# Inverting unit triangles from 32x32 diagonal blocks on four PE positions, with the sums kept in PSUM and copied out by ScalarE

## The reference

```
def step(S, inp):                                   # rwkv7_scan, one token
    sa = einsum('bhij,bhj->bhi', S, a_t)
    S = S * w_t[:, :, None, :] + sa[..., None] * b_t[:, :, None, :] + v_t[..., None] * k_t[:, :, None, :]
    return S, einsum('bhij,bhj->bhi', S, r_t)

L = where(strict, einsum('bhnid,bhnjd->bhnij', kb, k) * decay, 0.0)      # gated_delta_chunked
t_inv = triangular_solve(eye + L, eye, left_side=True, lower=True, unit_diagonal=True)
u = t_inv @ (v * beta[..., None])
```

## Time and profile before

| | us |
|---|---|
| median of 3 runs | 2749.25 (2746.87 to 2752.73) |
| profiled execution, its own time | 2759.18 |
| its span | 2757.5 |
| PE busy | 2218.6 (80%) |
| DVE busy | 831.5 (30%) |
| ACT busy | 352.2 (13%) |
| mean granted TensorE clock | 0.854 |

### The profile page before, as it was taken

How to read it: one execution, slowest core, us unless ns; L and a number is a source line. 1 busy time by engine, 2 the same in 40 slices (tenths; PEclk the granted TensorE clock), 3 DMA queues, 4 the chain that set the end, 5 groups by cost and what they waited for, 6 DMA issues and landing times.

```text
span 2757.5 us, 37784 instructions
## 1 busy us (share of the span) xinstructions
PE 2218.6 (80%) x16019; PEld 1519.3 (55%) x16019; DVE 831.5 (30%) x1482; ACT 352.2 (13%) x771; POOL 191.2 (7%) x210
## 2 busy tenths in 40 slices
PE   5968888777687888889883998677787888898883
PEld 2445667666574555555552445566674555555551
DVE  1333333433534111111114353456544111111114
ACT  0012111111010111111110013200010111111110
POOL 0000000000000111111110000000000111111110
PEclk9965787877798999999996996588896999999996
DMA  8440233311223999999997152000013999999996
GB/s 296 141 126 7 117 123 127 123 62 62 42 47 143 371 381 370 380 382 366 388 373 280 61 161 84 1 1 9 6 39 126 371 380 374 372 384 370 374 369 243
DMA packets 129926, 581.35 MB, mean 211 GB/s; under 512 B 25890, under 2 KB 33052, under 8 KB 78424
## 3 DMA queue, kind: packets, MB, share of 16 engines
q1 hardware_dynamic: 88368, 496.07, 46.8%
q0 software_dynamic: 28480, 60.42, 6.5%
q10 hardware_dynamic: 12904, 22.35, 2.7%
HBM read 566.42 MB, written 48.30 MB: 223 GB/s over the span
## 4 chain that ended last, share of the span: by engine, by line
PE 62%; DMA 20%; DVE 12%; issue 2%; ACT 1%; PEldq 1%; SPq 1%; PEld 1%; ACTq 0%; DVEq 0%; POOL 0%; POOLq 0%
PE bank L552 57%; DMA ring<-in_exp_w_up 12%; DVE arena L1512 7%; DMA ring<-in_exp_w_down 3%; DMA ring<-in_mod_w 2%; DMA arena<-choice_rows 1%; PE bank L1033 1%; PE bank L656 1%; DMA ring<-in_ev_w_in 1%; DVE mixed L1512 1%; PE bank L1057 1%; DVE arena L1526 1%; DVE arena L1520 1%; PE bank L749 1%; PEld bank L552 0%
## 5 line engine op out<-in xcount | busy, mean ns | idle before, releaser
L552 PE MATMUL bank<-ring,arena 128*64 128x256 f32 (+3 forms) x5168 | 944.2, 447 | 138.5 <-DMA ring<-in_exp_w_up 87.6
L552 PEld LDWEIGHTS bank<-ring,arena 128*64 128x64 f32 (+1 forms) x5168 | 575.2, 158 | 470.4 <-issue 364.6
L552 PE MATMUL bank<-arena 64*64 64x64 f32 (+8 forms) x6176 | 435.2, 257 | 64.0 <-DVE arena L1512 42.1
L552 PEld LDWEIGHTS bank<-arena 64*64 64x64 f32 (+5 forms) x6176 | 376.4, 163 | 103.0 <-DVE arena L1512 41.9
L1526 DVE COPY arena<-bank 128x512 f32<-128x512 f32 (+4 forms) x231 | 151.6, 663 | 562.9 <-PE bank L552 491.2
L552 PE MATMUL bank<-ring,hT 128*128 128x512 f32 (+2 forms) x672 | 265.6, 555 | 12.0 <-DMA ring<-in_ev_w_in 5.7
L1520 DVE SCALAR_TENSOR_TENSOR arena<-bank,arena 128x256 f32<-128x256 f32 (+1 forms) x84 | 40.1, 477 | 683.3 <-PE bank L552 683.3
L552 PEld LDWEIGHTS bank<-ring,hT 128*128 128x128 f32 x672 | 128.1, 199 | 148.7 <-issue 143.0
L2220 POOL DMA_INDIRECT arena<-token_rows,arena x80 | 80.6, 1008 | 940.7 <-PE bank L1033 658.2
L1512 DVE TENSOR_TENSOR arena<-arena 128x1024 f32<-128x1024 f32 (+7 forms) x135 | 124.2, 947 | 48.3 <-DMA arena<-choice_rows 34.7
L552 PE MATMUL bank<-hT,ring 128*128 128x384 f32 x384 | 127.2, 488 | 4.0 <-DVE arena L1512 2.3
(11 more groups left out here) (176 smaller groups left out, 1222.7 us busy)
## 6 DMA issues: line engine op xcount, KB each, us to landing
ring<-in_exp_w_gate SPq DMA_DIRECT2D x128, 1024.0 KB, 10.0
ring<-in_exp_w_up SPq DMA_DIRECT2D x128, 1024.0 KB, 9.6
ring<-in_exp_w_down SPq DMA_DIRECT2D x128, 1024.0 KB, 10.1
ring<-in_mod_w SPq DMA_DIRECT2D x48, 1024.0 KB, 10.2
ring<-in_od_w_in SPq DMA_DIRECT2D x14, 1024.0 KB, 9.9
arena<-choice_rows POOLq DMA_DIRECT2D x4, 3072.0 KB, 14.4
ring<-in_ev_w_in SPq DMA_DIRECT2D x10, 1024.0 KB, 14.8
arena<-arena ACTq DMA_DIRECT2D x12, 672.0 KB, 10.6
```

The lines of the kernel that those rows point to most:

```text
L552: return nc.tensor.matmul(out, lhsT, rhs, start=start, stop=stop, **kw)
```

## The change

Up to width 32 the inverse is now kept as 32x32 diagonal blocks: `low`, 128 partitions by 2 x 4 x 32, T and its transpose. Its products are 32x32 matmuls, 16 for four heads and four quarters of the partitions, and the four quarters sit on four positions of PE. Level 0 is two sums in PSUM (identity by a 128x256 matmul, plus the triangle's blocks by multiplying with a small identity), masked by VectorE. From level 1 on the sum T + join stays in PSUM (one identity matmul puts T there at level 1, the joins accumulate), and ScalarE copies it out to `low` at levels 1 to 4, so that VectorE's add is gone; VectorE's mask is half as wide. The level 32 to 64 becomes a corner of its own, as 64 to 128 was: it has no mask, one product, one join, and copies. Since tt and the new t64 are filled by blocks, POOL clears both whole, and VectorE copies the blocks of `low` into them; ScalarE writes the new corner for group 0, VectorE for group 1.

```diff
-LEVELS = 7
+LOW_LEVELS = 5
+M_STEPS, J_STEPS, T_STEPS = 6, 7, 8
+Q = 32
...
             def invert(inv, n, dirs):          # tensor program
...
+                for g in range(2):
+                    out = bank[2 + g][:, 0:8 * Q].rearrange("p (k h n) -> p k h n", k=2, h=4)
+                    pe.wait_ge(inv.sem("nt_ready", g), n + 1)
+                    mm(bank[2 + g][:, 0:8 * Q], C["ident"], small_ident.unsqueeze(1).broadcast_to([P, 8, Q]), True, False, **acc)
+                    for h in range(4):
+                        for r in QUARTERS:
+                            mm(out[r, 0, h, :], inv.nt[g][r, h, r], small_ident[r, :], False, True, **acc)
+                    for h in range(4):
+                        for r in QUARTERS:
+                            last = mm(out[r, 1, h, :], small_ident[r, :], inv.nt[g][r, h, r], False, True, **acc)
+                    last.then_inc(inv.sem("join_ready", g), 1)
+                for k in range(1, LOW_LEVELS):
                     for g in range(2):
+                        pe.wait_ge(inv.sem("t_ready", g), T_STEPS * n + k)
+                        if k == 1:
+                            mm(bank[2 + g][:, 0:8 * Q], C["ident"], inv.low[g].rearrange("p k h n -> p (k h n)"), True, False,
+                               **acc)
+                        for h in range(4):
+                            for r in QUARTERS:
+                                last = mm(bank[g][r, Q * h:Q * (h + 1)], inv.nt[g][r, h, r], inv.low[g][r, 0, h, :])
                         last.then_inc(inv.sem("m_ready", g), 1)
                     for g in range(2):
+                        pe.wait_ge(inv.sem("m_saved", g), M_STEPS * n + k)
...
+                                mm(out[r, 0, h, :], inv.low[g][r, 1, h, :], inv.m1_low[g][r, h, :], False, True, **acc)
...
+                                last = mm(out[r, 1, h, :], inv.m1_low[g][r, h, :], inv.low[g][r, 1, h, :], False, True, **acc)
                         last.then_inc(inv.sem("join_ready", g), 1)
                 for g in range(2):
+                    pe.wait_ge(inv.sem("t_ready", g), T_STEPS * n + LOW_LEVELS)
+                    for h in range(4):
+                        for p in HALVES:
+                            a, c = inv.inner(p, dirs[g])
+                            last = mm(bank[g][c, Q * h:Q * (h + 1)], inv.nt[g][a, h, c], inv.low[g][a, 0, h, :])
+                    last.then_inc(inv.sem("m_ready", g), 1)
+                for g in range(2):
+                    pe.wait_ge(inv.sem("m_saved", g), M_STEPS * n + LOW_LEVELS)
+                    for h in range(4):
+                        a, c = inv.inner(inv.corners(dirs[g])[0], dirs[g])
+                        mm(bank[4 + g][c, 128 + Q * h:128 + Q * (h + 1)], inv.low[g][c, 1, h, :], inv.m1_low[g][c, h, :])
+                        for p in HALVES:
+                            a, c = inv.inner(p, dirs[g])
+                            last = mm(bank[4 + g][a, Q * h:Q * (h + 1)], inv.m1_low[g][c, h, :], inv.low[g][c, 1, h, :])
+                    last.then_inc(inv.sem("join_ready", g), 1)
...
             def invert(inv, n, dirs):          # scalar program
+                for k in range(1, LOW_LEVELS):
+                    for g in range(2):
+                        act.wait_ge(inv.sem("join_ready", g), J_STEPS * n + k + 1)
+                        nc.scalar.copy(inv.low[g].rearrange("p k h n -> p (k h n)"), bank[2 + g][:, 0:8 * Q])\
+                            .then_inc(inv.sem("t_ready", g), 1)
+                for g in range(2):
+                    act.wait_ge(inv.sem("m_ready", g), M_STEPS * n + LOW_LEVELS)
+                    for p in HALVES:
+                        a, c = inv.inner(p, dirs[g])
+                        last = nc.scalar.copy(inv.m1_low[g][c, :, :], heads(bank[g][c, 0:4 * Q], 4))
+                    last.then_inc(inv.sem("m_saved", g), 1)
+                act.wait_ge(inv.sem("cleared", 0), n + 1)
+                act.wait_ge(inv.sem("join_ready", 0), J_STEPS * n + LOW_LEVELS + 1)
...
+                nc.scalar.copy(inv.t64[0][c, :, o:o + Q], heads(bank[4][c, 128:256], 4))
...
+                    last = nc.scalar.copy(inv.tt[0][a, :, c], heads(bank[4][a, 0:128], 4))
+                last.then_inc(inv.sem("t_ready", 0), 1)
...
+            def join(inv, n, dirs):            # vector program
+
+                for g in range(2):
+                    dve.wait_ge(inv.sem("join_ready", g), J_STEPS * n + 1)
+                    tt(inv.low[g].rearrange("p k h n -> p (k h) n"), heads(bank[2 + g][:, 0:8 * Q], 8),
+                       low_masks[0].unsqueeze(1).broadcast_to([P, 8, Q]), ALU.mult).then_inc(inv.sem("t_ready", g), 1)
+                for k in range(1, LOW_LEVELS):
                     for g in range(2):
+                        dve.wait_ge(inv.sem("m_ready", g), M_STEPS * n + k)
+                        tt(inv.m1_low[g], heads(bank[g][:, 0:4 * Q], 4), low_masks[k].unsqueeze(1).broadcast_to([P, 4, Q]),
                            ALU.mult).then_inc(inv.sem("m_saved", g), 1)
+                for g in range(2):
+                    dve.wait_ge(inv.sem("cleared", g), n + 1)
+                    dve.wait_ge(inv.sem("t_ready", g), T_STEPS * n + LOW_LEVELS)
+                    for r in inv.inner(inv.corners(dirs[g])[0], dirs[g]):
+                        o = r.start % 64
+                        copy(inv.t64[g][r, :, o:o + Q], inv.low[g][r, 0, :, :])
+                    for r in QUARTERS:
+                        last = copy(inv.tt[g][r, :, r], inv.low[g][r, 1, :, :])
+                    last.then_inc(inv.sem("t_ready", g), 1)
+                dve.wait_ge(inv.sem("join_ready", 1), J_STEPS * n + LOW_LEVELS + 1)
...
+                    nc.gpsimd.memset(inv.t64[g], 0.0)
+                    nc.gpsimd.memset(inv.tt[g], 0.0).then_inc(inv.sem("cleared", g), 1)
```

More of the change, by code:

```diff
@@ L102, in constants @@
     full[:, o + 80:o + 144] = np.where(j < SINGLES, SINGLES * i + j, PERIODS * SINGLES + 6 * i + j - SINGLES)
-    b = s % half
-    c = t[:, 0:half]
-    for k in range(LEVELS - 1):
-        full[:, o + 144 + half * k:o + 144 + half * (k + 1)] = (b >> (k + 1) == c >> (k + 1)) & (b >> k != c >> k)
-    full[:, o + 528:o + 592] = b == c
+    b = s % Q
+    c = t[:, 0:Q]
+    for k in range(LOW_LEVELS):
+        full[:, o + 144 + Q * k:o + 144 + Q * (k + 1)] = (b >> (k + 1) == c >> (k + 1)) & ((k == 0) | (b >> k != c >> k))
+    full[:, o + 304:o + 336] = b == c
     full[:, o + 8:o + 72] = (np.arange(GROUPS)[None, :] < np.arange(GROUPS)[:, None]).reshape(-1)
@@ L366, in corners, with inner @@
                 return (low, high) if d == 0 else (high, low)
+            def inner(self, p, d):
+                first, second = slice(p.start, p.start + Q), slice(p.start + Q, p.stop)
+                return (first, second) if d == 0 else (second, first)
             def sem(self, name, g):
@@ L680, in invert @@
             def invert(inv, n, dirs):
[L681 to L692 removed]
+                acc = dict(skip_group_check=True)
@@ L1728, in attend @@
                 end_phase()
-            def join(inv, n):
-                for k in range(LEVELS - 1):
+            def join(inv, n, dirs):
[4 more added lines that the diff above has]
+                for k in range(1, LOW_LEVELS):
@@ L1751, in rwkv @@
+                dve.wait_ge(inv.sem("join_ready", 1), J_STEPS * n + LOW_LEVELS + 1)
+                a, c = inv.inner(inv.corners(dirs[1])[0], dirs[1])
+                o = a.start % 64
+                copy(inv.t64[1][c, :, o:o + Q], heads(bank[5][c, 128:256], 4))
+                for p in HALVES:
+                    a, c = inv.inner(p, dirs[1])
+                    last = copy(inv.tt[1][a, :, c], heads(bank[5][a, 0:128], 4))
+                last.then_inc(inv.sem("t_ready", 1), 1)
             def rwkv():
@@ L1800, in rwkv @@
                         last.then_inc(sem("gram_saved"), 1)
[L1801 removed]
+                    join(r_inverse, u, (d, d))
                     dve.wait_ge(sem("y_unit_ready"), u + 1)
@@ L1914, in delta @@
                             tt(d_rs[g], v, beta, ALU.mult).then_inc(sem("rs_ready"), 1)
-                    join(d_inverse, len(RWKV_UNITS) + n)
+                    join(d_inverse, len(RWKV_UNITS) + n, [d for _, d in step])
                     for g, (t, d) in enumerate(step):
```

88 lines of the change are left out of this document (33 added, 55 removed).

## The result

| | before | changed |
|---|---|---|
| median, us | 2748.06 (2736.87 to 2752.73, 4 runs) | 2812.41 (2801.11 to 2819.66, 4 runs) |
| ratio, with its 95% interval | | 1.0235 [1.0196, 1.0274] |
| profiled span, us | 2757.5 | 2809.2 |
| mean granted TensorE clock | 0.854 | 0.820 |

What follows compares the result with a forecast made beforehand. The nine inversions, bound by PE and its waits, were to lose 31 us in six even-layer ones and 22 in three odd-layer ones, together 53 us. Against the median of 2749.25 that gave 2696 us, range 2678 to 2740.

Steps and rivals of the forecast that it cites:

- What bounds the kernel: Nine inversions, 239.0 us together, run with nothing else waited for; their gain or loss enters the time one for one.
- The price of a record: One 32x32 matmul record on PE costs 10 ns at full clock, between 7.5 and 15 ns.
- The rule that I set against it: Matmul start-to-start never below about 25 ns: 4.8 us a level, inversions 41 us longer, 2790 us.
- Part 1, level 0: Start of each inversion: level 1's 32x32 part starts at 4.3 us, 4.6 before; nearly nothing won.
- Part 2, levels 2 to 4: Inversion levels 2 to 4 take 2.24 us each against 3.34; the 32-wide corner starts at 13.9 us.
- Part 3, the new corner: 32-to-64 corner: first chain ready at 16.4 us, second's copies end at 18.1, inversion ends at 20.3 against 25.5.
- Rival (a): PE's records are limited by instruction fetch: a level takes 3.2 us, 28 us won, 2721 us; chance 0.18.
- Rival (b): PE's clock falls to 1.2 GHz in inversions: 2.83 us a level, 23 us won, 2726 us; chance 0.14.
- Rival (c): A record costs 29 ns whatever its width: 5.6 us a level, 2824 us; chance 0.13 for any price above 20 ns.
- Rival (d): The new corner's small copies and waits eat the levels' gain, 27 of 28 us given back: 2748 us; chance 0.05.

Runs made afterwards that it cites:

- the loop: Changed kernel with PE's levels 1 to 4 looped: at 8.4 ns the first loop, 2786.07 us; at 83 us the clean loop, 2729.36 us.
- the quarter version: Changed kernel with four heads in one 32x128 matmul at levels 0 to 4, a quarter of the instructions, some products left out: 2691.99 us.
- the clean loop: Changed kernel with PE's levels 1 to 4 as a loop whose waits use the loop variable, without extra one-column matmuls: 2729.36 us, 0.9953 of the kernel before.
- `e10_loop_less`: The clean loop with level 0's transposed half in 4 matmuls of 32x128 a chain instead of 16 of 32x32: 2718.70 us, 0.9896 of the kernel before.
- the first loop: Changed kernel with PE's levels 1 to 4 as a loop, each wait carried by an extra one-column matmul: 2786.07 us, 1.0168 of the kernel before.
- 64-column matmuls: Changed kernel, no loop, with two heads in one 32x64 matmul at levels 0 to 4, half the instructions, some products left out: 2719.57 us.
- the extra matmuls: Kernel before, unrolled, with 32 unused one-column matmuls of 32x32 weights added behind each level's join: 2774.94 us.

## Why the prediction was wrong

The sum took PE's instructions to be there whenever PE wants them, at twice the old pace. They were not, and the rest of the sum held.

- **What bounds the kernel** held: the inversions stand alone, and what they lost (56.8 us) is what the span lost (51.7).
- **The price of a record**, 10 ns, held: 9.6 ns over 170 records in the changed kernel, 8.4 over 32 in the loop. The line through two shapes had given 7.5, the nearest row 15. The rule that I set against it, from the Trainium skill ("TensorE: Matmul & The Clock Gate", section "Wait — 56ns, not 53.3ns?"), that start to start is never below some 25 ns, does not hold between matmuls on four positions, where these 8.4 and 9.6 ns stand. Its 2790 came within 22 us of the measured time by chance.
- **Part 1, level 0** held: the 32-wide part of level 1 starts 4.6 us in (295.46 to 300.05), 4.3 were forecast.
- **Part 2, levels 2 to 4, is the step that failed**: "Sum 2.24 us against 3.34". The sum has PE's records, ScalarE's copy and the waking, and takes it that 384 instructions are there when PE wants them. They come in 5.8 us, and in the first inversion levels 2 to 4 take 17.0 us where 6.7 were forecast. With the feed taken away the sum is right: 1.97 us in the quarter version, 2.30 in the clean loop less its jump (2.65 - 0.35).
- **Part 3, the new corner** held at the full clock, but for VectorE's copies. In the changed kernel's first inversion it takes 9.4 us (from the end of ScalarE's copy at 319.56 to 328.95) where 6.4 were forecast: 1.5 of the 3 us is the pause ahead of 320.83, and the rest falls in a stretch whose clock is 0.50. In the clean loop the corner starts at 309.96 (the level's start at 307.66 and PE's 2.3 us), the first chain is ready 2.4 us later (2.5 forecast), the second 3.65 (4.2), the end at 316.31 6.35 (6.4). The twelve small copies are faster than taken, 0.23 us each and not 0.28. The clean loop's timeline:

```profile
309.88 2.77 DVE L1586 COPY arena<-arena 32x128 f32<-32x128 f32 x12 [1.11 <-ACT arena L1341]
...
312.40 0.67 PE L564 MATMUL bank<-arena 64*64 64x64 f32 x8 [0.41 <-ACT arena L1356]
...
313.61 0.96 PE L564 MATMUL bank<-arena 64*64 64x64 f32 x16 [0.54 <-DVE arena L1586]
```

- **Rival (a) named the mechanism**, at a chance of 0.18, with a size that no row had shown: 1.0 us for the transfer and one more for the rest. A block takes 3.87 on average. The rows gave two ends for it: 1.0 us, the packet's own time, and 4.45 us, the pace at which the kernel before was fed without a stall (4.2 in the prediction, which took 243 instructions a fetch; they are 256). Only the second is a bound; at 4.45 a level would be 6.7 us, 3.3 more than before, and the nine inversions' levels 2 to 4 alone 90 us longer. I read "no such stall at the old pace" as speaking against the rival, and it says nothing at a pace twice as high. My own rule for a price that no row shows, to keep both ends for the range, would have put some 2840 into it.
- The Trainium skill has the block ("Runtime: NRT & Kernel Launch", section "Instruction fetch mechanics"): 16 KiB, 256 instructions, fetched while the one before is executed. The 16.4 KB a fetch and the pauses at 256 agree. That crossing a block is mostly hidden does not hold here: 1.5 to 2.5 us of each 3.9 are standing time.
- **Rival (b), the clock**, came too, 0.60 for 0.90. It isn't the cause of the loss in the levels: the first pause stands at a granted clock of 1.00, and in the third inversion of the last loop (`e10_loop_less`) a level of the same records at 0.50 takes 3.47 us (450.77 to 454.24), where the changed kernel's take 5.7. But it costs in the corner, some 1.5 us in the first inversion; nine times that, 13 us, is my estimate for all. With the pauses gone the clock is 0.84 to 0.90 in the quarter version, and with three of them left 0.77 to 0.89 in the clean loop, but 0.60 to 0.68 in the first loop, so standing still is not its only cause, and what else takes it is open.
- **Rival (c)** forecast 2824 and the time is 2812; the 29 ns that it took for the price of a record lie by chance beside the 30 ns at which a record and its weight load are fed. That is luck, the right number with the wrong reason: it would have said that a loop is useless, and the loop gave 83 us in the windows.
- **Rival (d)** did not come: in the clean loop the small copies cost no more than taken.

## What to carry to other kernels

Count the instructions of a stage, not only its work: a stage of small matmuls whose rows show no "issue" can still be just under the rate at which code arrives, and halving the tile and doubling the count brings it over. A stage that wants 256 instructions in less than some 4 us, for longer than the code in hand lasts, is a case for a loop, or for fewer and wider instructions; the loop took 83 us off the changed kernel's inversions and nothing off the kernel before. A resource whose rate of use grows is to be priced between its shortest transfer and the pace that was seen to do, and the second end belongs in the range.

## What the runs showed of the hardware

- A block of 256 PE instructions comes every 3.45 to 4.0 us in three kernels that ran out of code (3.45 with 64-column matmuls, 3.73 with the extra matmuls, 3.87 on average in the changed kernel). PE's pauses stand 128 matmul records apart, and the fetches in the trace keep the same pace.
- A loop of 384 to 400 instructions, more than one block, runs from its second turn on without fetching (no instruction transfer from 302.0 to 310.8 in the clean loop); the jump back costs 0.31 to 0.37 us.
- fp32 matmuls of 32x32 on four positions start 8.4 to 9.6 ns apart at the full clock.
- A full-array matmul of one column between 32-wide groups costs PE some 0.4 us at the full clock.
- The granted clock can fall to 0.50 without a pause of PE: in the first loop, busy with 32-wide groups and one-column matmuls, at about 310.6. A level of that loop takes 3.70 us at the full clock and 5.36 at the low one.
- Code that is due earlier can simply be waited for longer: level 1 moved forward by 1.5 us met a pause of 2.2.
